# Per-head RMS norm and rotation of q and k: Sqrt and reciprocal replaced by Ln, Exp and one Newton step

## The chip, the core and the metric

The kernel runs on one core of one Trainium2 chip. The metric is device time of one execution in microseconds (us), lower is better. PE is TensorE, DVE is VectorE, ACT is ScalarE, POOL is GpSimd, SP is SyncE, which here only issues DMAs.

## What is computed

One encoder block: modulated RMS norm, an input projection, grouped-query attention beside a Fourier branch, gates, an output projection, then a GeGLU MLP. The change touches only the norm and rotation of q and k, which in the reference are:

```python
def rms_norm(x, g):
    xf = x.astype(jnp.float32)
    y = xf * lax.rsqrt(jnp.mean(xf * xf, axis=-1, keepdims=True) + NORM_EPS)
    return (y * g.astype(jnp.float32)).astype(x.dtype)
...
        h = rms_norm(x, mix_pre_g[l]) * (1.0 + scale1) + shift1
        z = h @ w_in[l]
        q = z[..., :o1].reshape(B, S, N_Q_HEADS, HEAD_DIM)
        k = z[..., o1:o2].reshape(B, S, N_KV_HEADS, HEAD_DIM)
...
        q = apply_rope(rms_norm(q, q_norm_g[l]), cos, sin)
        k = apply_rope(rms_norm(k, k_norm_g[l]), cos, sin)
```

There are 2048 positions, 8 query heads and 2 key heads of 64 channels, so q and k are 640 channels: 5 chunks of 128 channels (two heads each), each in 4 blocks of 512 positions. That is 20 blocks of 128x512 F32.

## The kernel before

`proj_phase` begins with six chunks of the projection: chunks 0 to 4 are q and k, chunk 5 is v. Then come 16 chunks of gates. PE makes a block by 24 matmuls of 128x512 (8 slices of the contraction, each a three-term hi/lo product, `product3`, L91 to L93) into one of four PSUM banks `ps[n]`. Block `i` is position block `n = i % 4` of chunk `c = i // 4`. For each of the 20 blocks of q and k the engines then do, in a pipeline whose order is written out by hand and whose joints are semaphores:

- ACT copies the block, times the gain, to `zg` (L888) and its square to `sq` (L889). It waits for the block's last product (`s_mm`) and, as `zg`, `sq`, `std` and `rot` have two slots each, for the end of block `i-2` (`s_rot`). With `hi_part` (L864), once a chunk, it rounds the weights of the next chunk.
- SP waits for `s_zg` and copies `zg` with neighbouring channels exchanged to `rot` by two DMAs (L693).
- PE takes the mean over each head's 64 channels by one F32 product with `head_mean` into `ps_ms` (L1017). It stands in PE's queue just ahead of the products of block `i+2`, and waits for `sq` and for the end of block `i-2`.
- ACT takes the root of mean + eps to `std` (`root`, L870, after the copies of block `i+1`).
- DVE multiplies by sin and cos and adds (L945, L946, L948), inverts `std` by a reciprocal (L950), makes the low part of the block before (L932, `rotated_lo`), and multiplies rotation and inverse root into `out` (L956), which posts `s_rot`. Once a chunk, L928 makes the low part of the next weights (`lo_part`).
- ACT rounds `out` of block `i-2` to `hi_st` (L876, `rotated_hi`), and POOL's queue stores both parts (L761, L763, `s_st`).

After block 19 ACT copies the four blocks of v (L907) into the buffers `out`, each when the stores from it have landed. PE turns them (L1038) and goes on with the gates, whose Sigmoids (L917) empty its PSUM banks.

Of the kernel before, what the change touches and what calls it, by code (L numbers as in the profile page):

```python
# [21 lines left out]
ALU = mybir.AluOpType  # L22
ACT = mybir.ActivationFunctionType
# [7 lines left out]
BLK = 512  # L31
NB = S // BLK
# [9 lines left out]
EPS = 1e-6  # L42
# [568 lines left out]
def proj_phase(nc, ahead, t_pos, w_z, w0, w0_at, hT_hi, hT_lo, b_gate, qk_g, rope_cos, rope_sin, head_mean_d, ident, f_d, f_stored, qk_d, gates_d,  # L611
# [7 lines left out]
    NROPE = NB * (NQC + 1)  # L619
# [6 lines left out]
    with Res(nc, "proj") as r:  # L626
        w_st, w_hi, w_lo = ([first] for first in w0)
        w_st.append(r.sb("w_st1", [P, KD, P]))
        for n, w in (("hi", w_hi), ("lo", w_lo)):
            r.sb(f"room_of_w_{n}0", [P, KD, P])  # L630
            w.append(r.sb(f"w_{n}1", [P, KD, P], F32R))
        out = r.sb("out", [P, NB, BLK])
# [13 lines left out]
        zg, sq, std, rot = (side[:, a, b * 2 * BLK:(b + 1) * 2 * BLK].rearrange("p (s q) -> p s q", s=2)  # L646
                            for a in (2, 3) for b in (0, 1))
# [3 lines left out]
        ps_ms = r.ps("ps_ms", [P, 2, BLK])  # L651
        ps_sw = r.ps("ps_sw", [P, 2, BLK])
        ps_m = [ps_ms, ps_sw, ps_b]
        ps = [ps_a[:, 0, :], ps_a[:, 1, :], ps_b[:, 0, :], ps_b[:, 1, :]]
        s_c, s_rt, s_eps = r.sem("consts"), r.sem("rotation_tables"), r.sem("eps_written")
        s_w = [r.sem(f"w_loaded{i}") for i in range(2)]
        s_hi, s_lo, s_mm, s_zg, s_ms, s_std, s_rot, s_out, s_rope = (
            r.sem(n) for n in ("w_hi_made", "w_lo_made", "products", "zg_sq", "mean", "root", "rotated", "v_or_gate", "rope"))
        s_sw = [r.sem(f"pairs_swapped{i}") for i in range(2)]
        s_rhi, s_rlo = r.sem("rotated_hi"), r.sem("rotated_lo")  # L660
        s_f, s_dft, s_z, s_zst = (r.sem(n) for n in ("f_loaded", "dft_steps", "z_split", "z_stored"))
# [5 lines left out]
        s_st = [r.pool_dma_sem(f"rotated_stored{n}") for n in range(NB)]  # L667
# [4 lines left out]
        for m in range(NG * NU):  # L672
            g, i = divmod(m, NU)
            n, k = divmod(i // UNITS * GROUPS_OF[g] * KD // -(-NU // UNITS), KD)
            units[NB * PER * g + FIRST_OF[g] + n][k].append(m)

        with r.block() as block:
# [182 lines left out]
            @block.scalar  # L860
            def _(act):
                def hi_part(c, i, u):
                    act.wait_ge(s_w[u], 16 * i + 16 * u)
                    act.activation(w_hi[u][:], w_st[u][:], ACT.Copy).then_inc(s_hi, 1)  # L864

                def root(c, n):
                    act.wait_ge(s_ms, 4 * c + n + 1)
                    if c or n >= 2:
                        act.wait_ge(s_rot, 4 * c + n - 1)
                    act.activation(std[:, n % 2, :], ps_ms[:, n % 2, :], ACT.Sqrt, bias=eps[:, 0:1]).then_inc(s_std, 1)  # L870

                def rotated_hi(i):
                    if i == 0:
                        f_stored(act)
                    act.wait_ge(s_rot, i + 1)
                    act.activation(hi_st[:, i % NB, :], out[:, i % NB, :], ACT.Copy).then_inc(s_rhi, 1)  # L876

                act.wait_ge(s_c, 16 * 3)
                act.wait_ge(s_eps, 1)
                for c in range(NQC + 1):  # L880
                    if c:
                        act.wait_ge(s_mm, 4 * c)
                    hi_part(c + 1, (c + 1) // 2, (c + 1) % 2)
                    for n in range(NB):
                        act.wait_ge(s_mm, 4 * c + n + 1)
                        if c or n >= 2:
                            act.wait_ge(s_rot, 4 * c + n - 1)
                        act.activation(zg[:, n % 2, :], ps[n], ACT.Copy, scale=gains[:, c:c + 1])  # L888
                        act.activation(sq[:, n % 2, :], ps[n], ACT.Square).then_inc(s_zg, 1)  # L889
                        if c or n >= 2:  # L890
                            rotated_hi(4 * c + n - 2)
                        if n:
                            root(c, n - 1)
                    root(c, NB - 1)

                def next_hi(c):
                    act.wait_ge(s_mm, 4 * c)
                    hi_part(c + 1, (c + 1) // 2, (c + 1) % 2)

                next_hi(NQC + 1)  # L900
                rotated_hi(NROPE - 2)
                for n in range(NB):
                    if n == 1:
                        rotated_hi(NROPE - 1)
                    act.wait_ge(s_mm, 4 * (NQC + 1) + n + 1)
                    act.wait_ge(s_st[n], STORED)
                    act.activation(out[:, n, :], ps[n], ACT.Copy).then_inc(s_out, 1)  # L907
                for j in range(2 * KD):
                    if NQKV + j + 1 < NC:
                        next_hi(NQKV + j)  # L910
                    for n in range(NB):
                        act.wait_ge(s_mm, 4 * (NQKV + j) + n + 1)
                        if j == 0:
                            act.wait_ge(s_tr, n + 1)
                        else:
                            act.wait_ge(s_gst[n], 16 * j)
                        act.activation(out[:, n, :], ps[n % 2], ACT.Sigmoid, bias=bg[:, j:j + 1]).then_inc(s_out, 1)  # L917
                        if j == 2 * KD - 1 and n == 2:
                            act.wait_ge(ahead.s_tp, 16)
                            act.wait_ge(s_un, NG * NU)  # L920
                            for k in range(ahead.K):
                                ahead.table_hi(act, k)

            @block.vector
            def _(dve):
                def lo_part(c, u):
                    dve.wait_ge(s_hi, c)
                    dve.tensor_tensor(w_lo[u][:], w_st[u][:], w_hi[u][:], ALU.subtract).then_inc(s_lo, 1)  # L928

                def rotated_lo(i):  # L930
                    dve.wait_ge(s_rhi, i + 1)
                    dve.tensor_tensor(out[:, i % NB, :].bitcast(F32R), out[:, i % NB, :], hi_st[:, i % NB, :],  # L932
                                      ALU.subtract).then_inc(s_rlo, 1)

                dve.memset(eps[:], EPS).then_inc(s_eps, 1)
                dve.wait_ge(s_rt, 16 * 2)
                for c in range(NQC + 1):
                    lo_part(c + 1, (c + 1) % 2)
                    for n in range(NB):
                        cols = slice(n * BLK, (n + 1) * BLK)  # L940
                        i = 4 * c + n
                        done = 4 * i
                        zc, rc, sc = zg[:, n % 2, :], rot[:, n % 2, :], std[:, n % 2, :]
                        dve.wait_ge(s_sw[n % 2], 32 * (i // 2 + 1))
                        dve.tensor_tensor(rc, rc, sin[:, cols], ALU.mult).then_inc(s_rope, 1)  # L945
                        dve.tensor_tensor(zc, zc, cos[:, cols], ALU.mult).then_inc(s_rope, 1)  # L946
                        dve.wait_ge(s_rope, done + 2)
                        dve.tensor_tensor(rc, rc, zc, ALU.add).then_inc(s_rope, 1)  # L948
                        dve.wait_ge(s_std, 4 * c + n + 1)
                        dve.reciprocal(sc, sc).then_inc(s_rope, 1)  # L950
                        if c or n:
                            rotated_lo(4 * c + n - 1)
                        dve.wait_ge(s_rope, done + 4)
                        if c:
                            dve.wait_ge(s_st[n], 32 * c)
                        dve.tensor_tensor(out[:, n, :], rc, sc, ALU.mult).then_inc(s_rot, 1)  # L956
                lo_part(NQKV, 0)
                rotated_lo(NROPE - 1)

                def split_v(n):  # L960
# [39 lines left out]
            def _(pe):  # L1000
# [10 lines left out]
                def rope_products(c, n):  # L1011
                    if c == 0 and n == 0:
                        pe.wait_ge(s_c, 16 * 3)
                    pe.wait_ge(s_zg, 4 * c + n + 1)
                    if c or n >= 2:
                        pe.wait_ge(s_rot, 4 * c + n - 1)
                    pe.matmul(ps_ms[:, n % 2, :], head_mean, sq[:, n % 2, :], start=True, stop=True).then_inc(s_ms, 1)  # L1017

                for c in range(NQC + 2):
                    if c:  # L1020
                        pe.wait_ge(s_lo, c)
                    for n in range(NB):
                        if c:
                            pe.wait_ge(s_zg, 4 * (c - 1) + n + 1)
                        if c <= NQC and n >= 2:
                            rope_products(c, n - 2)
                        if c and n < 2:
                            rope_products(c - 1, n + 2)
                        block_products(n, c % 2, n)
# [31 lines left out]
                for j in range(2 * KD):  # L1061
                    pe.wait_ge(s_lo, NQKV + j)
                    for n in range(NB):
                        i = NB * j + n
# [2196 lines left out]
```

## Time and profile before

| | |
|---|---|
| Median of 3 runs | 3081.8 us (3079.35 to 3087.96) |
| The profiled execution's own time | 3081.74 us |
| Its span | 3079.9 us |
| PE busy | 3002.9 us, 98% of the span |
| DVE busy | 2370.0 us, 77% |
| ACT busy | 1451.9 us, 47% |
| POOL busy | 574.8 us, 19% |
| Stage of q and k | first product at 160.3 us, last mean product at 298.9 us |

The time is 1.8 us more than the span, the stretch from the first to the last instruction. Busy times are sums over the whole span, and say nothing on a single stage. In the rows further down, the number after an instruction's start is its duration, and what stands in brackets is the engine's idle time before it and what ended it.

### The profile page before, as it was taken

How to read it: one execution, taken by the hardware profiler on the slowest of the kernel's cores; microseconds unless marked ns; L12 is line 12 of the kernel's file. 1: busy time of each engine (PE TensorE's matmuls, PEld its weight loads, DVE VectorE, ACT ScalarE, POOL GpSimd, SP SyncE). 2: the span in 40 equal slices, each digit the busy share in tenths (PEclk: the TensorE clock that was granted, in tenths of full speed). 3: DMA queues.
4: the chain of work that ended last, by engine and by line, in shares of the span. 5: the costliest groups of instructions: out<-in, count | busy, mean ns of one | idle time of the engine just before them, and what ended most of it. 6: DMA issues, size and time to landing. Idle time of an engine off the chain costs nothing.

```text
span 3079.9 us, 35419 instructions
## 1 busy us (share of the span) xinstructions
PE 3002.9 (98%) x13417; PEld 2418.7 (79%) x13417; DVE 2370.0 (77%) x2302; ACT 1451.9 (47%) x1856; POOL 574.8 (19%) x513
## 2 busy tenths in 40 slices
PE   5999999999999999999999999999999999999998
PEld 4777777777788888877888778888888888888887
DVE  6679687776499999997566789999564899996453
ACT  5433111111799999983333444444343444444433
POOL 0011522532000000000000244443120444440000
PEclk9999999999999999999999999999999999999999
DMA  8643332223721111148666332222664222226663
GB/s 338 216 150 135 130 112 80 86 100 124 228 52 38 35 39 35 39 128 248 188 218 218 132 110 82 82 83 82 218 215 166 93 82 83 82 83 218 215 211 126
DMA packets 159322, 408.11 MB, mean 133 GB/s; under 512 B 17992, under 2 KB 38472, under 8 KB 154664
## 3 DMA queue, kind: packets, MB, share of 16 engines
q1 hardware_dynamic: 141472, 352.88, 35.2%
q0 software_dynamic: 10192, 36.18, 3.1%
q10 hardware_dynamic: 7488, 16.78, 1.4%
q8 instruction: 107, 1.75, 0.2%
q14 instruction: 63, 0.52, 0.1%
HBM read 296.51 MB, written 104.02 MB: 130 GB/s over the span
## 4 chain that ended last, share of the span: by engine, by line
PE 66%; DVE 4%; ACT 1%; DMA 1%; issue 1%; POOL 0%; SPq 0%; ACTq 0%; DVEq 0%; POOLq 0%
PE second_ps_a L91 8%; PE second_ps_a L93 8%; PE second_ps_a L92 8%; PE second_ps_b L91 8%; PE second_ps_b L93 8%; PE second_ps_b L92 8%; PE att_ps_o L1597 7%; PE att_ps_s L1582 4%; PE att_ps_s L1583 4%; PE att_ps_r L1610 2%; DMA merge_x<-in_w_out 1%; PE att_ps_r L1615 0%; PE second_ps_b L1841 0%; DVE att_prob_lo L1519 0%; DVE ffn_x L2925 0%
## 5 line engine op out<-in xcount | busy, mean ns | idle before, releaser
L1519 DVE TENSOR_TENSOR att_prob_lo<-att_prob,att_prob_hi 128x1024 fp32r<-128x1024 f32 x256 | 309.9, 1221 | 24.1 <-ACT att_prob_hi L1479 22.9
L91 PE MATMUL second_ps_a<-up_in_hi,up_wu_hi 128*128 128x512 f32 x728 | 284.0, 390 | 5.1 <-DVE up_wu_lo L2375 3.1
L2911 DVE TENSOR_TENSOR ffn_wd_lo<-ffn_wd_st,ffn_wd_hi 128x1024 fp32r<-128x1024 f32 x110 | 130.6, 1224 | 201.9 <-ACT ffn_wd_hi L2734 201.9
L93 PE MATMUL second_ps_a<-up_in_hi,up_wu_lo 128*128 128x512 f32 x728 | 283.3, 389 | 0.0
L92 PE MATMUL second_ps_a<-up_in_lo,up_wu_hi 128*128 128x512 f32 x728 | 283.3, 389 | 0.0
L1479 ACT ACTIVATE att_prob_hi<-att_prob 128x1024 fp32r<-128x1024 f32 x256 | 272.2, 1064 | 0.0
L1473 ACT ACTIVATE att_prob<-att_ps_s 128x1024 f32<-128x1024 f32 x256 | 262.4, 1026 | 9.9 <-PE att_ps_s L1583 9.9
L2734 ACT ACTIVATE ffn_wd_hi<-ffn_wd_st 128x1024 fp32r<-128x1024 f32 x110 | 110.8, 1052 | 243.1 <-PE second_ps_a L93 132.1
L917 ACT ACTIVATE proj_out<-proj_ps,proj_bg 128x512 f32<-128x512 f32 x64 | 44.1, 689 | 378.2 <-PE proj_ps L93 365.5
L1597 PE MATMUL att_ps_o<-att_prob_hi,heads_kv 128*128 128x512 f32 x512 | 200.1, 391 | 1.8 <-DVE att_prob_lo L1519 1.7
L1597 PE MATMUL att_ps_o<-att_prob_lo,heads_kv 128*128 128x512 f32 x512 | 199.4, 389 | 0.0
L91 PE MATMUL second_ps_b<-up_in_hi,up_wu_hi 128*128 128x512 f32 x504 | 196.2, 389 | 0.0
L93 PE MATMUL second_ps_b<-up_in_hi,up_wu_lo 128*128 128x512 f32 x504 | 196.1, 389 | 0.0
L92 PE MATMUL second_ps_b<-up_in_lo,up_wu_hi 128*128 128x512 f32 x504 | 196.1, 389 | 0.0
L2015 POOL DMA_DIRECT2D scratch_x<-second_y x16 | 9.9, 620 | 966.0 <-DVE second_y L2199 966.0
L91 PEld LDWEIGHTS second_ps_a<-up_in_hi,up_wu_hi 128*128 128x128 f32 x728 | 136.6, 188 | 34.7 <-DVE up_wu_lo L2375 3.9
L93 PEld LDWEIGHTS second_ps_a<-up_in_hi,up_wu_lo 128*128 128x128 f32 x728 | 136.6, 188 | 28.5
L92 PEld LDWEIGHTS second_ps_a<-up_in_lo,up_wu_hi 128*128 128x128 f32 x728 | 136.7, 188 | 28.2
L2698 ACT ACTIVATE ffn_cv<-ffn_u,ffn_cw 128x1025 f32<-128x1025 f32 x88 | 109.8, 1248 | 99.3 <-issue 79.5
L91 PE MATMUL second_ps_b<-ffn_wd_hi,ffn_gs 128*128 128x512 f32 x396 | 154.3, 390 | 1.7 <-DVE ffn_gs L2907 1.7
L1533 DVE TENSOR_TENSOR att_acc<-att_acc,att_prob 128x1024 f32<-128x1024 f32 x128 | 155.9, 1218 | 0.0
L92 PE MATMUL second_ps_b<-ffn_wd_lo,ffn_gs 128*128 128x512 f32 x396 | 154.1, 389 | 0.0
(352 smaller groups left out, 8180.5 us busy)
## 6 DMA issues: line engine op xcount, KB each, us to landing
ffn_wd_st<-in_w_dn SPq DMA_DIRECT2D x110, 512.0 KB, 4.9
up_w_st<-in_w_up SPq DMA_DIRECT2D x44, 512.0 KB, 3.6
ffn_g_raw<-scratch_g SPq DMA_DIRECT2D x88, 192.0 KB, 4.2
scratch_gates<-proj_out SPq DMA_DIRECT2D x64, 256.0 KB, 2.0
early_w_st<-in_w_branch SPq DMA_DIRECT2D x32, 512.0 KB, 7.0
merge_gate<-scratch_gates SPq DMA_DIRECT2D x64, 256.0 KB, 3.7
up_w_st<-in_w_up SPq DMA_DIRECT2D x44, 256.0 KB, 4.1
up_w_a<-in_w_up SPq DMA_DIRECT2D x44, 256.0 KB, 4.3
```

The costliest lines, as they stand in the source:

```text
L91: pe.matmul(out, w_hi, x_hi, start=first, stop=False)
L92: pe.matmul(out, w_hi, x_lo, start=False, stop=False)
L93: return pe.matmul(out, w_lo, x_hi, start=False, stop=last)
L1473: act.activation(prob[:, s % RING, :], ps_s[:, s % 3, :], ACT.Exp, scale=SCALE).then_inc(s_exp, 1)
L1479: act.activation(prob_hi[:, s % LAG, :], prob[:, s % RING, :], ACT.Copy).then_inc(s_hi, 1)
L1519: dve.tensor_tensor(prob_lo[:, s % LAG, :], prob[:, s % RING, :], prob_hi[:, s % LAG, :], ALU.subtract)\
L1533: dve.tensor_tensor(at, at, prob[:, s % RING, :], ALU.add).then_inc(s_add, 1)
L1582: pe.matmul(at, kv[h % 2][:, 0, keys], q1[h % 2][:, cols], start=True, stop=False)
L1583: m = pe.matmul(at, kv[h % 2][:, 2, keys], q2[h % 2][:, cols], start=False, stop=True)
L1597: m = pe.matmul(ps_o[:], v, src[:, s % LAG, j * BLK:(j + 1) * BLK], start=t == 0 and part == 0, stop=t == NT - 1 and part == 1)
L2734: act.activation(wd_hi[split_at(m)][:], wd_st[staged_at(m)][:], ACT.Copy).then_inc(s_dhi, 1)
L2911: dve.tensor_tensor(wd_lo[split_at(m)][:], wd_st[staged_at(m)][:], wd_hi[split_at(m)][:], ALU.subtract).then_inc(s_dlo, 1)
```

## The change

The inverse root no longer comes from Sqrt and reciprocal. ACT now takes Ln of the mean, Exp of -0.5 times that, y, and the square of y, each waiting for the one before it. DVE makes one Newton step, y (1.5 - 0.5 m y^2), in two instructions. As eps can no longer be Sqrt's bias, DVE adds it to each square ahead of the mean product. On ACT the mean's instructions now come ahead of `rotated_hi` of block `i-2`. On DVE, the inverse root and the final product of block `i-1` come ahead of the rotation of block `i`. `s_zg` is now posted by the copy; the squares have a semaphore of their own. The mean stays one F32 product.

```diff
-                def root(c, n):
-                    act.wait_ge(s_ms, 4 * c + n + 1)
-                    if c or n >= 2:
-                        act.wait_ge(s_rot, 4 * c + n - 1)
-                    act.activation(std[:, n % 2, :], ps_ms[:, n % 2, :], ACT.Sqrt, bias=eps[:, 0:1]).then_inc(s_std, 1)
+                def inverse_root(i):
+                    at = std[:, i % 2, :]
+                    act.wait_ge(s_ms, i + 1)
+                    act.activation(at, ps_ms[:, i % 2, :], ACT.Ln).then_inc(s_std, 1)
+                    act.wait_ge(s_std, 3 * i + 1)
+                    act.activation(at, at, ACT.Exp, scale=-0.5).then_inc(s_std, 1)
+                    act.wait_ge(s_std, 3 * i + 2)
+                    act.activation(sq[:, i % 2, :], at, ACT.Square).then_inc(s_std, 1)
...
                     for n in range(NB):
-                        act.wait_ge(s_mm, 4 * c + n + 1)
-                        if c or n >= 2:
-                            act.wait_ge(s_rot, 4 * c + n - 1)
-                        act.activation(zg[:, n % 2, :], ps[n], ACT.Copy, scale=gains[:, c:c + 1])
-                        act.activation(sq[:, n % 2, :], ps[n], ACT.Square).then_inc(s_zg, 1)
-                        if c or n >= 2:
-                            rotated_hi(4 * c + n - 2)
-                        if n:
-                            root(c, n - 1)
-                    root(c, NB - 1)
+                        i = NB * c + n
+                        act.wait_ge(s_mm, i + 1)
+                        if i >= 2:
+                            act.wait_ge(s_rot, i - 1)
+                        act.activation(zg[:, n % 2, :], ps[n], ACT.Copy, scale=gains[:, c:c + 1]).then_inc(s_zg, 1)
+                        act.activation(sq[:, n % 2, :], ps[n], ACT.Square).then_inc(s_sq, 1)
+                        if i:
+                            inverse_root(i - 1)
+                        if i >= 2:
+                            rotated_hi(i - 2)
+                inverse_root(NROPE - 1)
...
+                def squares_eps(i):
+                    at = sq[:, i % 2, :]
+                    dve.wait_ge(s_sq, i + 1)
+                    dve.tensor_scalar(at, at, EPS, None, ALU.add).then_inc(s_sqeps, 1)
...
+                def newton(i, step):
+                    root, square = std[:, i % 2, :], sq[:, i % 2, :]
+                    if step == 0:
+                        dve.wait_ge(s_std, 3 * i + 3)
+                        dve.scalar_tensor_tensor(square, square, -0.5, ps_ms[:, i % 2, :], ALU.mult, ALU.mult).then_inc(s_nr, 1)
+                    else:
+                        dve.wait_ge(s_nr, 2 * i + 1)
+                        dve.scalar_tensor_tensor(root, square, 1.5, root, ALU.add, ALU.mult).then_inc(s_nr, 1)
...
                 for c in range(NQC + 1):
                     lo_part(c + 1, (c + 1) % 2)
-                        dve.wait_ge(s_std, 4 * c + n + 1)
-                        dve.reciprocal(sc, sc).then_inc(s_rope, 1)
...
+                    for i in range(NB * c, NB * (c + 1)):
+                        squares_eps(i)
+                        if i:
+                            newton(i - 1, 0)
+                        if i >= 2:
+                            rotated_lo(i - 2)
+                        if i:
+                            newton(i - 1, 1)
+                            normed(i - 1)
+                        rotate(i)
...
-                    pe.wait_ge(s_zg, 4 * c + n + 1)
+                    pe.wait_ge(s_sqeps, 4 * c + n + 1)
```

`rotate` holds the three instructions of L945 to L948 and `normed` the one of L956.

The next two fences are ACT's queue in the stage of q and k, one block long, first before the change. `proj_side` stands for each of `zg`, `sq`, `std`, `rot`, `cos` and `sin`, which lie in one buffer.

```order
L888 ACTIVATE proj_side<-proj_ps,proj_gains 128x512 [waits proj_rotated,proj_products]
L889 ACTIVATE proj_side<-proj_ps 128x512
L876 ACTIVATE proj_hi_st<-proj_out 128x512 [waits proj_rotated]
L870 ACTIVATE proj_side<-proj_ps_ms,proj_eps 128x512 [waits proj_rotated,proj_mean]
L888 ACTIVATE proj_side<-proj_ps,proj_gains 128x512 [waits proj_rotated,proj_products]
```

And with the change (L893 and L894 are the copy and the square, L870 Ln, L872 Exp, L874 the second Square, L880 `rotated_hi`):

```order
L893 ACTIVATE proj_side<-proj_ps,proj_gains 128x512 [waits proj_rotated,proj_products]
L894 ACTIVATE proj_side<-proj_ps 128x512
L870 ACT_TABLE_LOAD
L870 ACTIVATE proj_side<-proj_ps_ms 128x512 [waits proj_mean]
L872 ACT_TABLE_LOAD
L872 ACTIVATE proj_side<-proj_side 128x512 [waits proj_root]
L874 ACTIVATE proj_side<-proj_side 128x512 [waits proj_root]
L880 ACTIVATE proj_hi_st<-proj_out 128x512 [waits proj_rotated]
L893 ACTIVATE proj_side<-proj_ps,proj_gains 128x512 [waits proj_rotated,proj_products]
```

Four instructions became eight: besides Exp and Square the compiled program holds a table load ahead of Ln and another ahead of Exp, in each of the 20 blocks, and `rotated_hi` moved behind them.

DVE's queue over one block before the change (L932 is `rotated_lo`):

```order
L945 TENSOR_TENSOR proj_side<-proj_side 128x512 [waits proj_pairs_swapped0]
L946 TENSOR_TENSOR proj_side<-proj_side 128x512
L948 TENSOR_TENSOR proj_side<-proj_side 128x512 [waits proj_rope]
L950 RECIPROCAL proj_side<-proj_side 128x512 [waits proj_root]
L932 TENSOR_TENSOR proj_out<-proj_out,proj_hi_st 128x512 [waits proj_rotated_hi]
L956 TENSOR_TENSOR proj_out<-proj_side 128x512 [waits proj_rope]
```

And with it (L946 now adds eps, L961 and L964 are the Newton step, L937 `rotated_lo`, L971 the final product, L952 to L955 the rotation):

```order
L946 TENSOR_SCALAR proj_side<-proj_side 128x512 [waits proj_squares_steps]
L961 SCALAR_TENSOR_TENSOR proj_side<-proj_side,proj_ps_ms 128x512 [waits proj_root]
L937 TENSOR_TENSOR proj_out<-proj_out,proj_hi_st 128x512 [waits proj_rotated_hi]
L964 SCALAR_TENSOR_TENSOR proj_side<-proj_side 128x512 [waits proj_newton_steps]
L971 TENSOR_TENSOR proj_out<-proj_side 128x512 [waits proj_newton_steps,proj_rope]
L952 TENSOR_TENSOR proj_side<-proj_side 128x512 [waits proj_pairs_swapped1]
L953 TENSOR_TENSOR proj_side<-proj_side 128x512
L955 TENSOR_TENSOR proj_side<-proj_side 128x512 [waits proj_rope]
```

The reciprocal is gone, three instructions came in, and the final product of a block moved from behind its own rotation to ahead of the next block's.

## Rows read from the trace of the kernel before

**Rows 1.** The page: busy us, share of the span, instructions.

```profile
PE 3002.9 (98%) x13417; PEld 2418.7 (79%) x13417; DVE 2370.0 (77%) x2302; ACT 1451.9 (47%) x1856; POOL 574.8 (19%) x513
```

**Rows 2.** One chunk: us; PE, PEld, DVE, ACT, POOL busy; granted clock; DMA share, GB/s.

```profile
217.80:245.40 27.60, 26.05 (x106) 19.24 (x105) 26.52 (x26) 10.15 (x19) 4.34 (x8) 1.00 0.36 134
```

**Rows 3.** Waits, 155 to 326 us: waiter, releaser, total us, times, longest.

```profile
ACT proj_side L888 <- DVE proj_out L956: 79.2, 18, 7.1
...
PE proj_ps_ms L1017 <- ACT proj_side L889: 4.8, 10, 1.1
```

**Rows 4.** Timeline of DVE, one block: start us, us, instruction.

```profile
256.58 0.68 DVE L945 TENSOR_TENSOR proj_side<-proj_side 128x512 f32<-128x512 f32 x1
257.19 0.68 DVE L946 TENSOR_TENSOR proj_side<-proj_side 128x512 f32<-128x512 f32 x1
257.90 0.69 DVE L948 TENSOR_TENSOR proj_side<-proj_side 128x512 f32<-128x512 f32 x1
258.51 3.35 DVE L950 RECIPROCAL proj_side<-proj_side 128x512 f32<-128x512 f32 x1
261.78 0.63 DVE L932 TENSOR_TENSOR proj_out<-proj_out,proj_hi_st 128x512 fp32r<-128x512 f32 x1
262.32 0.68 DVE L956 TENSOR_TENSOR proj_out<-proj_side 128x512 f32<-128x512 f32 x1
```

**Rows 5.** Timeline of ACT over the same block.

```profile
255.62 0.69 ACT L888 ACTIVATE proj_side<-proj_ps,proj_gains 128x512 f32<-128x512 f32 x1 [4.64 <-DVE proj_out L956]
256.21 0.59 ACT L889 ACTIVATE proj_side<-proj_ps 128x512 f32<-128x512 f32 x1
256.69 0.63 ACT L876 ACTIVATE proj_hi_st<-proj_out 128x512 fp32r<-128x512 f32 x1
257.21 0.69 ACT L870 ACTIVATE proj_side<-proj_ps_ms,proj_eps 128x512 f32<-128x512 f32 x1
263.09 0.69 ACT L888 ACTIVATE proj_side<-proj_ps,proj_gains 128x512 f32<-128x512 f32 x1 [5.20 <-DVE proj_out L956]
```

**Rows 6.** Timeline of PE: mean products of blocks 0, 5 and 19.

```profile
171.29 1.02 PE L1017 MATMUL proj_ps_ms<-proj_side,proj_small 128*128 128x512 f32 x2
...
202.86 1.02 PE L1017 MATMUL proj_ps_ms<-proj_side,proj_small 128*128 128x512 f32 x2
...
298.85 1.10 PE L1017 MATMUL proj_ps_ms<-proj_side,proj_small 128*128 128x512 f32 x2 [0.16 <-ACT proj_side L889]
```

**Rows 7.** Timeline of ACT at a table load elsewhere, in the MLP.

```profile
1767.31 0.58 ACT L2679 ACTIVATE ffn_p<-second_ps_a 128x512 f32<-128x512 f32 x1
1767.91 1.28 ACT L2704 ACT_TABLE_LOAD   x1
1769.20 1.06 ACT L2704 ACTIVATE ffn_cv<-ffn_cv 128x1025 f32<-128x1025 f32 x1
```

**Rows 8.** Groups by line and shape: count, busy us, mean ns.

```profile
L1825 DVE TENSOR_SCALAR second_y<-second_y,second_stats 128x1024 f32<-128x1024 f32 x10 | 7.0, 750 | 0.0
L2940 DVE SCALAR_TENSOR_TENSOR ffn_x<-ffn_y_g,ffn_rstd,ffn_x 128x512 f32<-128x512 f32 x2 | 1.4, 750 | 0.0
```

**Rows 9.** Timelines at the stage's begin: ACT's copy of block 1, DVE's first low part.

```profile
171.49 0.69 ACT L888 ACTIVATE proj_side<-proj_ps,proj_gains 128x512 f32<-128x512 f32 x1 [2.80 <-PE proj_ps L93]
...
171.70 1.23 DVE L928 TENSOR_TENSOR proj_w_lo<-proj_w_st,proj_w_hi 128x1024 fp32r<-128x1024 f32 x1 [11.31 <-DMA proj_side<-in_rope_sin]
```

**Rows 10.** Timelines behind the stage: last final product, v, first Sigmoid, v turned.

```profile
310.03 0.68 DVE L956 TENSOR_TENSOR proj_out<-proj_side 128x512 f32<-128x512 f32 x1
...
322.53 0.60 ACT L907 ACTIVATE proj_out<-proj_ps 128x512 f32<-128x512 f32 x1 [6.57 <-DMA scratch_qk<-proj_out]
...
325.39 0.69 ACT L917 ACTIVATE proj_out<-proj_ps,proj_bg 128x512 f32<-128x512 f32 x1
...
327.54 0.60 PE L1038 MATMUL proj_ps_sw<-keep_ident,proj_out 128*128 128x128 f32 x4
```

**Rows 11.** Columns as in rows 2, for a stretch of the first phase.

```profile
60.00:80.00 20.00, 16.14 (x81) 13.17 (x80) 14.83 (x17) 15.56 (x25) 0.00 (x0) 0.91 0.53 185
```

More of the change, by code:

```diff
@@ L658, in proj_phase @@
             r.sem(n) for n in ("w_hi_made", "w_lo_made", "products", "zg_sq", "mean", "root", "rotated", "v_or_gate", "rope"))
+        s_sq, s_sqeps, s_nr = (r.sem(n) for n in ("squares_steps", "squares_eps", "newton_steps"))
         s_sw = [r.sem(f"pairs_swapped{i}") for i in range(2)]
@@ L936, in _, with rotate @@
                 dve.wait_ge(s_rt, 16 * 2)
+                def squares_eps(i):
+                    at = sq[:, i % 2, :]
+                    dve.wait_ge(s_sq, i + 1)
+                    dve.tensor_scalar(at, at, EPS, None, ALU.add).then_inc(s_sqeps, 1)
+                def rotate(i):
+                    cols = slice(i % NB * BLK, (i % NB + 1) * BLK)
+                    zc, rc = zg[:, i % 2, :], rot[:, i % 2, :]
+                    dve.wait_ge(s_sw[i % 2], 32 * (i // 2 + 1))
+                    dve.tensor_tensor(rc, rc, sin[:, cols], ALU.mult).then_inc(s_rope, 1)
+                    dve.tensor_tensor(zc, zc, cos[:, cols], ALU.mult).then_inc(s_rope, 1)
+                    dve.wait_ge(s_rope, 3 * i + 2)
+                    dve.tensor_tensor(rc, rc, zc, ALU.add).then_inc(s_rope, 1)
@@ L937, in _, with normed @@
+                def normed(i):
+                    dve.wait_ge(s_rope, 3 * i + 3)
+                    dve.wait_ge(s_nr, 2 * i + 2)
+                    if i >= NB:
+                        dve.wait_ge(s_st[i % NB], 32 * (i // NB))
+                    dve.tensor_tensor(out[:, i % NB, :], rot[:, i % 2, :], std[:, i % 2, :], ALU.mult).then_inc(s_rot, 1)
                 for c in range(NQC + 1):
                     lo_part(c + 1, (c + 1) % 2)
[L939 to L948, printed above, removed]
-                        dve.wait_ge(s_std, 4 * c + n + 1)
-                        dve.reciprocal(sc, sc).then_inc(s_rope, 1)
[L951 to L956, printed above, removed]
@@ L957, in _ @@
+                    for i in range(NB * c, NB * (c + 1)):
[8 more added lines that the diff above has]
+                        rotate(i)
                 lo_part(NQKV, 0)
+                newton(NROPE - 1, 0)
+                rotated_lo(NROPE - 2)
@@ L958, in _ @@
+                newton(NROPE - 1, 1)
+                normed(NROPE - 1)
                 rotated_lo(NROPE - 1)
@@ L1013, in rope_products @@
                         pe.wait_ge(s_c, 16 * 3)
-                    pe.wait_ge(s_zg, 4 * c + n + 1)
+                    pe.wait_ge(s_sqeps, 4 * c + n + 1)
                     if c or n >= 2:
                         pe.wait_ge(s_rot, 4 * c + n - 1)
-                    pe.matmul(ps_ms[:, n % 2, :], head_mean, sq[:, n % 2, :], start=True, stop=True).then_inc(s_ms, 1)
+                    at = ps_ms[:, n % 2, :]
+                    pe.matmul(at, head_mean, sq[:, n % 2, :], start=True, stop=True).then_inc(s_ms, 1)
                 for c in range(NQC + 2):
@@ L1023, in _ @@
                         if c:
-                            pe.wait_ge(s_zg, 4 * (c - 1) + n + 1)
+                            pe.wait_ge(s_sq, 4 * (c - 1) + n + 1)
                         if c <= NQC and n >= 2:
```

## The prediction

> **What bounds the kernel now.** I read the page first: PE is busy for 98% of the span [rows 1], so a change away from PE pays or costs only where PE comes to wait for it. Then the stretches: over one chunk of q and k (27.60 us) PE is busy 26.05, DVE 26.52 and ACT 10.15 [rows 2]. This is the only stage in which DVE is as full as PE. The waits say who is late. ACT's copy of a block waits 18 times, 79.2 us in all, for DVE's final product two blocks back, and PE waits 10 times, 4.8 us, for the squares that ACT makes behind that copy [rows 3]. The reader is to see a ring in rows 4 and 5: DVE's final product of a block lets ACT start on the block after the next, and DVE goes from that product straight to the next rotation. Its queue sets the pace: 0.61 for the sin product, 0.71, 0.61, then 3.27 for the reciprocal, 0.54 and 0.60, start to start, about 6.34 us for a block, and with the waits for the root and one `lo_part` a chunk 27.6/4 = 6.90 [rows 2, 4]. PE by itself is only a little faster: mean product 0 starts at 171.29 and product 5 at 202.86, so PE unhindered needs 6.31 us a block; the last starts at 298.85 [rows 6]. At PE's own pace it would start at 171.29 + 19 x 6.31 = 291.2. So 7.7 us is all that any change of this stage can gain. A measurement of this kernel can tell about 0.3% (9.2 us) from no change, so "faster" is nearly out of reach before the change is looked at.
>
> **DVE gets lighter.** The reciprocal goes (3.27 of queue). Three instructions come in. Two are SCALAR_TENSOR_TENSOR on 128x512. The nearest rows are 0.68 for a two-input product and 0.75 for this operation with a scalar read from memory [rows 4, 8]; the scalars here are immediates, so I take 0.72, with 0.68 and 0.75 as ends. The third adds eps, TENSOR_SCALAR 128x512. The row is 0.75 for 128x1024, so between half of that, 0.38, and the 0.68 of the two-input product. I take 0.45, since a fixed part doesn't halve. Queue time per block: 6.34 - 3.27 + 2 x 0.63 + 0.36 = 4.7 us. DVE is no longer the bound, by 1.6 us against PE.
>
> **ACT gets two table loads a block.** ACT's queue with the change has a load before Ln and one before Exp, 40 in all; the trace of before has none in this stage. The row elsewhere shows what one costs: the instruction ahead ends at 1767.89, the load starts at 1767.91, takes 1.28, and the next starts at 1769.20 [rows 7]. So 1.29 for the load, 0.02 for the wait until the engine has run dry, and the overlap of about 0.1 between neighbours (0.58 start to start for an instruction of 0.69 [rows 5]) is lost too. The load doesn't wait for data, so it could hide in idle time. But both stand between ACT's squares of block `i` and DVE's Newton step of block `i-1`, and the ring runs through just there.
>
> A rule of the Trainium skill speaks of this price ("ScalarE: Activation LUTs", What ACT_TABLE_LOAD costs): 1283 ns for the load and some 1380 ns of drain, 2.66 us for every switch to another set. The trace agrees on the 1.28 and not on the drain: 0.02 us after the end of what stood ahead. By the page's price the sum below would be higher by 2 x 1.38 x 18 = 50 us.
>
> **The ring, step by step.** Start T(i) is ACT's copy of block `i`. DVE's iteration `i` ends the ring with the final product of block `i-1`, for which ACT's copy of block `i+1` waits. From rows 4, 5 and 7:
>
> - copy, 0.58 to the next start, and square, 0.59: 1.17
> - dry, 0.02, and first load, 1.29: 2.48
> - Ln of 128x512 out of PSUM. Square with the same operands takes 0.59, Sqrt with a pointer for its bias 0.69; no pointer shows in the queue, so 0.59: 3.07. Its mean is long there, as that product runs behind the products of block `i`.
> - dry and second load, 1.31: 4.38
> - Exp, from SBUF, as the 0.63 of L876: 5.01
> - 0.04 for a dependence inside the engine (L948 starts 0.03 after the end of L946 [rows 4]; I allow up to 0.1). Square, 0.63, and 0.03 to DVE, by the same row: 5.71
> - first Newton instruction, 0.63 to the next start: 6.34. By then `rotated_hi`, which starts 0.52 behind the second Square, is done too (6.21).
> - `rotated_lo`, 0.54: 6.88
> - second Newton instruction, 0.72 + 0.03: 7.63
> - final product, 0.68, and 0.10 to ACT (262.32 + 0.68 to 263.09 [rows 4, 5]): 8.41
>
> The ends: 8.3 with 0.68 for the Newton instructions and no dependence cost; 8.65 with Ln at 0.69, Newton at 0.75 and 0.1 for each dependence. The rest hides. `hi_part`, some 1.05 a chunk, fits in ACT's idle time from 6.2 to 8.4. Rotation, `lo_part` and eps add on DVE (1.93 + 1.13 + 0.36) are done 3.3 us after T, while DVE waits for ACT until 5.7. PE needs 6.31 of 8.41, so it now waits about 2.1 us a block, at its mean product, for the eps add.
>
> So a period of 8.41 in place of 6.90. PE gained with the reciprocal what it can't use, and the loads take it back twice over: without them the ring would be 8.41 - 2.6 = 5.8, below PE's 6.31.
>
> **The sum.** T(1) stays at 171.49 [rows 9]; block 1 hangs on PE alone. T(19) = 171.49 + 18 x 8.41 = 322.9. The first mean product is late, as eps add 0 stands behind `lo_part`, which waits for the rotation tables until 171.70 [rows 9]: 171.70 + 1.13 + 0.45 + 0.08 = 173.4 in place of 171.29, 2 us of PE time. That runs beside the ring and costs at most 0.4 there. Mean product 19 waits for rotation 18 and eps add 19: 322.9 + 1.75 + 0.45 + 0.08 = 325.2, against 298.85 [rows 6]. **Late by 26.3 us.**
>
> Behind it PE runs as before: blocks of v, first gates. The slack there gets smaller. The last final product now ends at about T(19) + 15.4 = 338.3 (two more loads, `hi_part` and `lo_part` stand before it), 27.6 later than 310.71, so 1.3 more than PE. The first Sigmoid ended at 326.08, while PE had turned the second block of v at 328.14 [rows 10]. Of these 2.1 us 1.3 go, and 0.8 is left. If it isn't, up to 3 us are lost. From there on everything moves by the same amount, for PE bounds the rest.
>
> Against the profiled execution's own 3081.74 us, which is the median to 0.1: 3081.7 + 26.3 = **3108.0 us**. The ring's ends move it by 18 x (-0.11 to +0.24) = -2 to +4.3, the slack by up to +3, the scatter of the runs of before (3079.4 to 3088.0) by some 3 to either side: 3101 to 3117.
>
> **Rivals.**
>
> *The loads are not what the chip does twice a block (other side, not slower).* If Ln and Exp lay in one table set that also serves Copy and Square, a single load would stand at the stage's begin. The ring would be 5.8, PE the bound at 6.31, and the last mean product at 173.4 + 19 x 6.31 = 293.3: 5.6 us gained, 3076, within 0.3%. It decides from a ring below 6.9 us, that is with fewer than 1.5 us of loads in it; with one load a block the ring is 7.1, and the time 3086. For it: only the names of the functions. Against it: the program of the change holds 40 loads, and those that the trace of before shows stand where its program has them. 3%, and 1% for the one load a block.
>
> The Trainium skill has the rule ("ScalarE: Activation LUTs", Table sets: the hidden batching unit): the set `natural_log_exp_and_others` has both, so Ln and then Exp cost one load. By it this rival would hold; no run of before shows either function beside the other.
>
> *The switch is dearer when it goes to and fro.* All loads in the trace stand alone, with long stretches between. If two in quick turn cost a further 1.38 each, the period is 11.2 and the time 3108 + 50 = 3158. For it no row of this trace; against it, the load itself has one length, 1.28 [rows 7]. 3%.
>
> *PE's clock falls.* PE will be busy for three quarters of this stage, with a gap in each block. In a stretch of the first phase with 16.14 busy of 20 us the granted clock was 0.91, so part of it ran at 1.2 GHz [rows 11]; at 0.94 busy it was 1.00 [rows 2]. A short fall is covered by PE's 2.1 us a block. If the clock stayed at 1.2 GHz, PE would need 2 x 6.31 = 12.6 a block and be the bound: 19 x 4.2 = 80 us on top, 3188. 3%.
>
> **Chances.** The forecast, two loads a block in a ring of 8.3 to 8.65, has 90% and gives 3101 to 3117. Rivals as said: 4% for fewer loads (within 0.3%), 3% for dearer switches, 3% for the clock. Since the smallest of the slower cases is 19 us off, three times the scatter, slower by over 0.3% has 0.95, within 0.3% 0.04, faster 0.01. The range takes one more us at each end for joints of ACT that no row shows: 3100 to 3118.
>
> **What would show it.** Table loads: 40 of 1.28 us between the first product and the v blocks, each starting 0.02 after the instruction ahead. Copies of ACT 8.4 us apart, waiting for the final product. DVE busy under 20 us in 34 and waiting on the second Square. PE waiting about 2 us a block at the mean product. No TABLE_LOAD there, or a period under 7, would prove me wrong in the main step; a period near 11 would give the second rival, and a clock under 0.8 with PE always busy the third.

## The result, and the profile after

The changed kernel takes 3114.3 us (median of 4 runs, 3111.7 to 3115.6) against 3081.1 us before: a ratio of 1.0094, with an interval of 1.0082 to 1.0106, so slower by 25 to 33 us. The quotient of these two medians is 1.0108 (33.2 us) and lies just outside that interval: with 4 runs to a side the size is less sure than the direction. Measured again, it took 3111.7 us (4 runs) against 3084.0 (15 runs), ratio 1.0087, 1.0071 to 1.0102. The forecast of 3081.7 + 26.3 us is a ratio of 1.0085, inside both intervals; 3114.3 is inside the range too, and 6 us above the number given.

The page of the changed kernel, its span and busy times:

```profile
span 3113.6 us, 35525 instructions
...
PE 3006.3 (97%) x13417; PEld 2420.5 (78%) x13417; DVE 2338.3 (75%) x2342; ACT 1527.5 (49%) x1936; POOL 570.3 (18%) x513
```

PE does the same 13417 matmuls. ACT has 76 us more, of which the loads are 51, and DVE 32 us less: work was taken from the engine that was full, and the kernel got slower. The same 27.6 us stretch as in [rows 2], columns as there:

```profile
217.80:245.40 27.60, 22.02 (x90) 16.30 (x89) 16.48 (x27) 20.98 (x28) 3.36 (x7) 1.00 0.29 105
```

PE fell from 26.05 us busy to 22.02, DVE from 26.52 to 16.48, and ACT rose from 10.15 to 20.98. No engine is full: this is what a ring of waits (each engine waits for another, and the last for the first) looks like in sums. The timeline of ACT over one block (start us, us, instruction), to be held against [rows 5]:

```profile
255.76 0.69 ACT L893 ACTIVATE proj_side<-proj_ps,proj_gains 128x512 f32<-128x512 f32 x1 [2.28 <-DVE proj_out L971]
256.35 0.59 ACT L894 ACTIVATE proj_side<-proj_ps 128x512 f32<-128x512 f32 x1
256.95 1.28 ACT L870 ACT_TABLE_LOAD   x1
258.25 0.60 ACT L870 ACTIVATE proj_side<-proj_ps_ms 128x512 f32<-128x512 f32 x1
258.86 1.28 ACT L872 ACT_TABLE_LOAD   x1
260.16 0.63 ACT L872 ACTIVATE proj_side<-proj_side 128x512 f32<-128x512 f32 x1
260.82 0.63 ACT L874 ACTIVATE proj_side<-proj_side 128x512 f32<-128x512 f32 x1
261.36 0.61 ACT L880 ACTIVATE proj_hi_st<-proj_out 128x512 fp32r<-128x512 f32 x1
261.88 1.05 ACT L865 ACTIVATE first_w_hi<-h_w_st 128x1024 fp32r<-128x1024 f32 x1
264.25 0.69 ACT L893 ACTIVATE proj_side<-proj_ps,proj_gains 128x512 f32<-128x512 f32 x1 [1.33 <-DVE proj_out L971]
```

Copy to copy is 8.49 us. The weights' part at 261.88 only shortens ACT's idle time, from 2.28 to 1.33. DVE's half of a ring, one block (the last row lets ACT start at 213.28):

```profile
206.53 0.42 DVE L946 TENSOR_SCALAR proj_side<-proj_side 128x512 f32<-128x512 f32 x1
210.51 0.69 DVE L961 SCALAR_TENSOR_TENSOR proj_side<-proj_side,proj_ps_ms 128x512 f32<-128x512 f32 x1 [3.56 <-ACT proj_side L874]
211.12 0.68 DVE L937 TENSOR_TENSOR proj_out<-proj_out,proj_hi_st 128x512 fp32r<-128x512 f32 x1
211.72 0.68 DVE L964 SCALAR_TENSOR_TENSOR proj_side<-proj_side 128x512 f32<-128x512 f32 x1
212.49 0.69 DVE L971 TENSOR_TENSOR proj_out<-proj_side 128x512 f32<-128x512 f32 x1
```

In this block DVE waits 3.56 us for ACT's second Square. The waits of the stage (155 to 356 us), in place of [rows 3]:

```profile
DVE proj_side L961 <- ACT proj_side L874: 60.6, 19, 3.6
...
ACT proj_side L893 <- DVE proj_out L971: 37.4, 18, 2.3
```

Each waits for the other once a block, ACT less than before (37.4 us for 79.2), DVE 60.6 us in 19 waits, 3.2 each. PE's mean products 0 and 19, for [rows 6]:

```profile
172.56 1.10 PE L1050 MATMUL proj_ps_ms<-proj_side,proj_small 128*128 128x512 f32 x2 [1.79 <-DVE proj_side L946]
...
326.00 1.10 PE L1050 MATMUL proj_ps_ms<-proj_side,proj_small 128*128 128x512 f32 x2 [1.75 <-issue]
```

The last one starts 27.15 us later than before (326.00 - 298.85). The spans differ by 33.7.

### The profile page after: what moved, and what is told of

Its sections match the earlier page's. It is cut to its first block, busy times and chain, and to the rows that moved or that the text cites. A ratio compares the mean times of both kernels' runs of the same rounds, so it can differ in the third digit from the quotient of the medians.

```text
span 3113.6 us, 35525 instructions
## 1 busy us (share of the span) xinstructions
PE 3006.3 (97%) x13417; PEld 2420.5 (78%) x13417; DVE 2338.3 (75%) x2342; ACT 1527.5 (49%) x1936; POOL 570.3 (18%) x513
## 4 chain that ended last, share of the span: by engine, by line
PE 66%; DVE 4%; ACT 1%; DMA 1%; issue 1%; POOL 0%; SPq 0%; ACTq 0%; DVEq 0%; POOLq 0%
PE second_ps_a L91 8%; PE second_ps_a L93 8%; PE second_ps_a L92 8%; PE second_ps_b L91 8%; PE second_ps_b L93 8%; PE second_ps_b L92 8%; PE att_ps_o L1630 7%; PE att_ps_s L1615 4%; PE att_ps_s L1616 4%; PE att_ps_r L1643 2%; DMA merge_x<-in_w_out 1%; PE att_ps_r L1648 0%; PE second_ps_b L1874 0%; DVE att_prob_lo L1552 0%; DVE ffn_x L2958 0%
## 5 line engine op out<-in xcount | busy, mean ns | idle before, releaser
L93 PEld LDWEIGHTS second_ps_a<-up_in_hi,up_wu_lo 128*128 128x128 f32 x728 | 136.6, 188 | 28.4
L92 PEld LDWEIGHTS second_ps_a<-up_in_lo,up_wu_hi 128*128 128x128 f32 x728 | 136.7, 188 | 28.4
L91 PE MATMUL second_ps_b<-ffn_wd_hi,ffn_gs 128*128 128x512 f32 x396 | 154.2, 389 | 1.7 <-DVE ffn_gs L2940 1.7
L93 PE MATMUL second_ps_b<-ffn_wd_hi,ffn_gs 128*128 128x512 f32 x396 | 154.1, 389 | 0.0
```

What stands on the lines that cost most here:

```text
L91: pe.matmul(out, w_hi, x_hi, start=first, stop=False)
L92: pe.matmul(out, w_hi, x_lo, start=False, stop=False)
L93: return pe.matmul(out, w_lo, x_hi, start=False, stop=last)
```

## The experiments

The theory is that the two loads stand on the ring. Its rivals are that the new order or the longer chain costs, or that the number of loads costs, wherever they are. Four kernels decide between them, and a fifth tests what one of them showed besides. The stage is read by the start of its last mean product.

**One set.** One load of the set that holds both functions, asked for by name at the head of the stage:

```diff
+                act.preload_act_table_set("natural_log_exp_and_others")
                 act.wait_ge(s_c, 16 * 3)
```

> The changed kernel with one added table load at the head of the stage of q and k, of the set that holds Ln and Exp together; no load stands in the blocks any more. Everything else, the eps add and the Newton step too, is as in the changed kernel. My theory (the two loads a block stand on the ring from ACT's copy to DVE's final product): the ring falls from 8.50 us by two times 1.31 and the regained overlap of 0.1 to about 5.8, under PE's own 6.31 us, so PE sets the pace. Last mean product at about 293 (298.9 before, 326.0 changed), time about 3076 us. Rival (the new order and the longer chain of ACT and DVE, not the loads, are what costs): the period stays above 6.9 and the time at or above that of before.

Measured: 3082.5 us (11 runs) against 3083.2 (33 runs), ratio 0.9989 (0.9979 to 1.0000). ACT over a block, no load in it:

```profile
250.97 0.69 ACT L894 ACTIVATE proj_side<-proj_ps,proj_gains 128x512 f32<-128x512 f32 x1 [2.80 <-PE proj_ps L93]
251.55 0.59 ACT L895 ACTIVATE proj_side<-proj_ps 128x512 f32<-128x512 f32 x1
252.03 0.60 ACT L870 ACTIVATE proj_side<-proj_ps_ms 128x512 f32<-128x512 f32 x1
252.66 0.63 ACT L872 ACTIVATE proj_side<-proj_side 128x512 f32<-128x512 f32 x1
253.33 0.63 ACT L874 ACTIVATE proj_side<-proj_side 128x512 f32<-128x512 f32 x1
...
257.28 0.69 ACT L894 ACTIVATE proj_side<-proj_ps,proj_gains 128x512 f32<-128x512 f32 x1 [2.80 <-PE proj_ps L93]
```

The copy now waits for PE, no longer for DVE: 6.31 us a block, PE's own pace. All of the slowdown is gone with the loads and nothing else changed, so neither the order nor the longer chain was the cause. The time missed its expectation of 3076 by 6.5 us. About 2 us of that are in the stage (294.96 in place of 293), at its begin:

```profile
173.27 1.93 PE L1051 MATMUL proj_ps_ms<-proj_side,proj_small 128*128 128x512 f32 x2 [2.78 <-DVE proj_side L947]
...
175.84 0.63 PE L93 MATMUL proj_ps<-h_hi,first_w_lo 128*128 128x512 f32 x1
176.27 0.63 PE L91 MATMUL proj_ps<-h_hi,first_w_hi 128*128 128x512 f32 x1
...
294.96 1.02 PE L1051 MATMUL proj_ps_ms<-proj_side,proj_small 128*128 128x512 f32 x2
```

PE had waited 2.78 us for the first eps add, and then ran for a while at 1.2 GHz: matmuls 0.43 us apart (175.84 to 176.27) in place of 0.23. A stretch of the same profile around it shows the granted clock at 0.66 (the number ahead of the DMA share):

```profile
172.00:177.00 5.00, 3.73 (x8) 2.30 (x9) 3.44 (x6) 1.71 (x3) 0.00 (x0) 0.66 0.26 98
```

That cost 1.7 us beside the wait: mean product 1 comes 8.05 after mean product 0 (181.32), not 6.31. The kernel with two idle loads, further down, shows the same: a wait of 2.43, the fall, and 8.00.

**One load a block on the ring.** The same call just ahead of each Ln, none at the head.

```diff
+                    act.preload_act_table_set("natural_log_exp_and_others")
                     act.wait_ge(s_ms, i + 1)
                     act.activation(at, ps_ms[:, i % 2, :], ACT.Ln).then_inc(s_std, 1)
```

> The changed kernel with the joint set of Ln and Exp loaded anew just ahead of each Ln: one load a block in place of two, at the same place of the ring. My theory (each load on the ring costs its whole 1.3 to 1.4 us a block): period 7.2 us, last mean product at about 303, time about 3086 us, halfway between none and two loads if the part below PE's pace is left out. Rival (a load hides behind something, or only the switch to and fro is dear): period at or below 6.9, or still near 8.5.

Measured: 3093.5 us (10 runs) against 3083.2, ratio 1.0032 (1.0022 to 1.0042). Two copies of ACT and what stands between them, shortened:

```profile
236.55 0.69 ACT L894 ACTIVATE proj_side<-proj_ps,proj_gains 128x512 f32<-128x512 f32 x1 [2.28 <-DVE proj_out L972]
...
237.75 1.28 ACT L869 ACT_TABLE_LOAD   x1
239.04 0.60 ACT L871 ACTIVATE proj_side<-proj_ps_ms 128x512 f32<-128x512 f32 x1
...
243.77 0.69 ACT L894 ACTIVATE proj_side<-proj_ps,proj_gains 128x512 f32<-128x512 f32 x1 [2.28 <-DVE proj_out L972]
```

The period is 7.22 us, the last mean product starts at 303.74, both as expected. From one load to two the period grows by 8.49 - 7.22 = 1.27. The whole missed its expectation of 3086 by 7.5 us. Against before it is 10.3 us slower, of which the stage has 4.9 (303.74 - 298.85); the other 5.4 are behind it (see below).

**Two loads a block in ACT's idle time.** One set, and behind `rotated_hi` in each block a load of another set and one back.

```diff
                         if i >= 2:
                             rotated_hi(i - 2)
+                        act.preload_act_table(ACT.Sigmoid)
+                        act.preload_act_table_set("natural_log_exp_and_others")
```

> As with one set for Ln and Exp, but with two loads in each block again, of another set and back, placed behind the part that rounds the rotated block, where ACT would be idle. As many loads as in the changed kernel (41 against 40), but off the ring. My theory: ACT's queue gets 6.15 us a block long, 6.4 with the weights' part, so the period is 6.3 to 6.5 and the time 3076 to 3081 us. Rival (what costs is the number of loads, wherever they stand): 26 us or more above before, as the changed kernel.

Measured: 3079.8 us (10 runs) against 3083.2, ratio 0.9985 (0.9976 to 0.9994). The loads are there, 41 in the stage where the changed kernel has 40, and ACT's queue has no gap left:

```profile
241.03 0.62 ACT L880 ACTIVATE proj_hi_st<-proj_out 128x512 fp32r<-128x512 f32 x1
241.66 1.28 ACT L900 ACT_TABLE_LOAD   x1
242.95 1.28 ACT L901 ACT_TABLE_LOAD   x1
244.25 1.06 ACT L865 ACTIVATE first_w_hi<-h_w_st 128x1024 fp32r<-128x1024 f32 x1
245.21 0.67 ACT L894 ACTIVATE proj_side<-proj_ps,proj_gains 128x512 f32<-128x512 f32 x1
```

The last mean product starts at 294.46, with one set at 294.96. So 51 us of table loads cost nothing in one place and 31 us of the stage (326.00 - 294.96) in another. The rival that counts loads falls.

**The order alone.** The new order with Sqrt (eps as bias) and reciprocal, no eps add, no Newton step.

```diff
-                        squares_eps(i)
...
+                    act.activation(std[:, i % 2, :], ps_ms[:, i % 2, :], ACT.Sqrt, bias=eps[:, 0:1]).then_inc(s_std, 1)
...
+                        dve.wait_ge(s_std, i + 1)
+                        dve.reciprocal(std[:, i % 2, :], std[:, i % 2, :]).then_inc(s_nr, 1)
```

> The order of the changed kernel (inverse root and final product of the block before come ahead of the rotation) with the old functions: Sqrt with eps as its bias and the reciprocal, no eps add, no Newton step. My theory: the reciprocal no longer waits for the root (0.47 us in half of the blocks before), and DVE's queue of 6.4 us a block plus the low part of the weights gives a period of 6.7 in place of 6.9; last mean product about 295, time about 3078 us, which is within the noise of before. Rival (the order costs): period above 6.9 and a longer time than before.

Measured: 3080.5 us (11 runs) against 3083.2, ratio 0.9989 (0.9978 to 0.9999). The last mean product started at 293.17, where that of before started at 298.85. DVE, from the low part of the weights on:

```profile
246.64 1.22 DVE L928 TENSOR_TENSOR first_w_lo<-h_w_st,first_w_hi 128x1024 fp32r<-128x1024 f32 x1
247.77 3.35 DVE L955 RECIPROCAL proj_side<-proj_side 128x512 f32<-128x512 f32 x1
251.04 0.63 DVE L932 TENSOR_TENSOR proj_out<-proj_out,proj_hi_st 128x512 fp32r<-128x512 f32 x1
```

The reciprocal starts as soon as DVE is free. The new order gains about 4 us of the stage by itself (this profile's stage also began 1.3 us earlier), so it can't be what made the change slow.

**eps in the Ln.** One set, and the eps add taken away: the late first mean product and the fall of the clock behind it should go with it.

```diff
-                        squares_eps(i)
...
-                    act.activation(at, ps_ms[:, i % 2, :], ACT.Ln).then_inc(s_std, 1)
+                    act.activation(at, ps_ms[:, i % 2, :], ACT.Ln, bias=eps[:, 0:1]).then_inc(s_std, 1)
...
-                        dve.scalar_tensor_tensor(square, square, -0.5, ps_ms[:, i % 2, :], ALU.mult, ALU.mult).then_inc(s_nr, 1)
+                        dve.scalar_tensor_tensor(square, ps_ms[:, i % 2, :], EPS, square, ALU.add, ALU.mult).then_inc(s_nr, 1)
```

> One table set for Ln and Exp, and no eps add on DVE: eps is Ln's bias and is added once more in the first Newton instruction; the second Square carries a factor of 0.5 and a sign moves to the final product, so DVE has three instructions of 0.69 where the kernel with one set has three and the add. Mean product 0 waits for ACT's squares alone again. My theory: no wait of 2.8 us at mean product 0 and no fall of PE's clock behind it, PE at its own 6.31 us from first to last: last mean product about 291 (295.0 with one set alone), time about 3 to 4 us under that of one set alone in the stage, some 7.5 us under before, about 3075 us. Rival (the pointer for the bias lengthens the ring past PE, or the clock falls anyway): no better than one set alone, some 3 us under before.

Measured: 3079.3 us (11 runs) against 3084.0 (15 runs), ratio 0.9982 (0.9973 to 0.9991): faster than both kernels, than that of before by only 0.2%. Its first and last mean product:

```profile
170.89 1.02 PE L1050 MATMUL proj_ps_ms<-proj_side,proj_small 128*128 128x512 f32 x2
...
290.84 1.02 PE L1050 MATMUL proj_ps_ms<-proj_side,proj_small 128*128 128x512 f32 x2
```

119.95 us for 19 blocks, 6.31 each, with no wait: the 7.7 us that the prediction called all that can be gained in this stage (127.56 before). Only 4.8 arrive in the medians.

**The same kernels again**, for the 6.6 us that the stage doesn't explain: a second profile of the changed kernel, a second and a third of before and of eps in the Ln.

> The changed kernel unchanged, for a second profile of it. The stage of q and k explains 27.1 of the 33.7 us by which the two profiles' spans differ. My theory for the other 6.6: falls of PE's granted clock at stage borders, which come and go from run to run and are not the change's; so the second profile has the same period of 8.50 us and the same 27 us in the stage, but other falls behind it, and another remainder. Rival (the change does something to the later stages): the same remainder of 6 to 7 us at the same places.

> The kernel before, for a second profile of it. If the falls of the granted clock come and go by themselves, this one has other falls behind the stage of q and k than the first, and its span differs from 3079.9 us by about 1.7 us for each stretch of half clock more or less. If they belong to the kernel, it has the same three.

> The kernel with eps in Ln once more, for its profile. In its first profile 8.1 us were gained by the end of the stage of q and k and only 2.4 by the end of the span; the clock fell at 767, 812, 1375 and 1426 us. If these falls come and go by themselves, the stage shows the same -8 us again and the rest other falls; if they belong to this kernel, the same ones stand there again and eat the same 5 to 6 us.

> The same kernel a third time, with the same two readings: the stage at -8 us in any case; the falls behind it the same as in the first profile if they belong to the kernel, others if they don't.

> The kernel before a third time, beside them. Its first two profiles had falls at 76, 1380 and 1431 us in common, the second two more at 1773 and 1804. If falls vary from run to run, the set differs again; by the other reading 76, 1380 and 1431 stay.

Measured: spans of 3113.6 and 3110.6 us for the changed kernel, 3079.9, 3084.0 and 3082.5 for that of before, 3077.5, 3078.6 and 3077.5 for eps in the Ln. The table gives how much later (+) than in the first profile of before the same DVE instruction starts, for instructions that stood at these times before:

| profile | 760 us | 1000 us | 1480 us | 2100 us | 3000 us |
|---|---|---|---|---|---|
| before, second | 0.1 | 0.2 | 0.2 | 4.3 | 4.1 |
| before, third | -0.2 | 1.2 | 1.8 | 2.7 | 2.6 |
| changed | 27.2 | 30.5 | 33.0 | 33.9 | 33.7 |
| changed, second | 28.4 | 31.3 | 29.4 | 30.9 | 30.7 |
| one set | -4.2 | -1.3 | 0.8 | 0.8 | 0.7 |
| one load | 4.9 | 5.5 | 9.1 | 12.0 | 11.9 |
| two idle loads | -4.7 | -4.5 | -4.4 | -4.4 | -4.1 |
| order alone | -5.7 | -5.8 | -8.9 | -7.4 | -7.5 |
| eps in the Ln | -8.3 | -5.4 | -2.2 | -2.2 | -2.5 |
| eps in the Ln, second | -4.3 | -1.5 | -3.6 | -1.2 | -1.4 |
| eps in the Ln, third | -8.7 | -5.9 | -5.5 | -2.5 | -2.4 |

The first column is the stage of q and k. (In the second profile of eps in the Ln it began 3.9 us later and took the same 120.0 us.) Behind it the kernel of before moves by 4.0 and 2.7 us against its own first profile; the changed kernel moves by 6.5 and 2.3, one load by 7.0, eps in the Ln by 5.8, 2.9 and 6.3. The profile that all are held against is the quietest of the three of before: behind the stage its clock fell twice (the very end aside), in the others four times each. Where time is lost, the clock often fell; a fall here is a stretch that the profile records at half the clock, 1.2 GHz. In the changed kernel's first profile, for instance, just behind the border to the Fourier stage:

```profile
800.00:810.00 10.00, 8.58 (x54) 8.39 (x55) 2.96 (x6) 2.66 (x5) 0.00 (x0) 0.83 0.83 294
```

The granted clock was 0.83 there; in the profile of before no fall is recorded between 80 and 1379 us. The falls behind the stage stood at 802, 846, 1410 and 1461 in the one profile of the changed kernel, at 846 and 1802 in the other; before had 1380 and 1431 each time, with 1773 and 1804 in the second, 773 and 1763 in the third. Eps in the Ln had 767, 812, 1375 and 1426 in the first, 814 and 1797 in the second, and in the third those of the first (766, 811, 1374, 1425) with 1756 and 1797. So part of them varies with the run and part comes again, and the two readings in the expectations are not told apart.

The steps of the table do go with the falls. Between 760 and 1000 us the clock fell in both profiles of the changed kernel, in one set and in all three of eps in the Ln, and each lost 2.8 to 3.3 us there. The third of before had one fall and lost 1.3. One load, two idle loads, order alone and the other two of before had none and moved by 0.6 or less. Ahead of every fall behind the stage PE had just waited 1.7 us or more, but for the one near 1380 (1410 in the changed kernel), where it had gaps of up to 1.0. Why such a place gets a fall in one run and not in another, and whether the change has a part in it, stays open: with two profiles of the changed kernel it can't be ruled out.

In the second profile of the changed kernel the clock also fell within the stage:

```profile
200.00:260.00 60.00, 49.71 (x185) 36.20 (x185) 35.70 (x59) 44.32 (x59) 7.55 (x14) 0.94 0.27 103
```

Its mean product 19 started 154.94 us after mean product 0, in the first profile 153.44. Five falls stand in that stretch, at 174, 218, 235, 269 and 303 us. The first cost the 1.5 us: mean product 1 came 8.00 after mean product 0, in the first profile 6.40. The next lap of the ring then waited for PE:

```profile
180.52 0.69 ACT L893 ACTIVATE proj_side<-proj_ps,proj_gains 128x512 f32<-128x512 f32 x1 [3.86 <-PE proj_ps L93]
```

The other four cost nothing, since the ring kept its 8.50 us a block: PE's waits covered them.

## Why the prediction was right

- **What bounds the stage.** Before, DVE's queue; no change of this stage could gain more than 7.7 us. Right: eps in the Ln reaches PE's pace and gains 7.6 (127.56 to 119.95).
- **DVE is lighter, and it is no use.** The Newton instructions took 0.69 (0.72 assumed), the eps add 0.42 (0.45). DVE was busy 16.48 of 27.6 us.
- **The loads' price.** 1.28 each, beginning 0.02 behind the instruction ahead, to and fro as well as alone. The period fell by 1.27 when one went. The 1380 ns of drain that the Trainium skill adds ("ScalarE: Activation LUTs", What ACT_TABLE_LOAD costs) appear in none of the 40; the rival with a dearer switch (3158 us) is out.
- **The ring.** 8.41 forecast, 8.50 measured. ACT's part is right to 0.02. The difference is on DVE: `rotated_lo` took 0.60 to the next start (0.54 assumed), and 0.77 passed between the second Newton instruction and the product, where 0.75 was assumed. Times 18 it is 1.6 us. As the stage also began 0.7 us earlier than before (its first product at 159.62 us), the last mean product was late by 27.15 and not by 27.9.
- **The first mean product** was late, by the wait of 1.79 us; in the first profile it cost the ring nothing to speak of, as forecast. What was missed is that the clock can fall behind such a wait. Where it fell there, block 1 took 1.6 to 1.7 us longer: in one set, with two idle loads, and also in the second profile of the changed kernel. "A short fall is covered by PE's 2.1 us a block" held for the four falls further on, not for this one.
- **PE's wait** was forecast for the eps add, at the mean product. PE waited at 17 mean products, 31.2 us in all; the profile puts 5 of these waits down to the eps add and names no releaser for the other 12.
- **Behind the stage** the first Sigmoid ended at 353.50 and PE had turned the second block of v at 355.28: 1.8 us of slack left, 0.8 forecast. Nothing was lost there.
- **The rival of the shared set** was priced rightly in the stage (last mean product 293.3 forecast, 294.96 measured, the clock between them), less so in the whole (3076 for 3082.5), and didn't hold for the kernel as built. With one load a block the prediction has a ring of 7.1 and 3086; its own sum gives 3084.4 for that ring, and the runs gave 7.22 and 3093.5. The Trainium skill is right that one set has both functions ("ScalarE: Activation LUTs", Table sets: the hidden batching unit); but the kernel gets it only when that set is asked for by name. From the names of the functions alone the loads alternated.
- **The size.** 3114.3 against 3108.0. The profile's 33.7 us are 7.4 more than the forecast: 0.8 of them lie in the stage (27.15 for 26.3), the other 6.6 behind it. Two of its four falls there (802 and 846) have no counterpart in the first profile of before, and the second profile of the changed kernel has only 2.3 us behind the stage. The second measurement (27.7 between the medians) is within 1.4 us of the forecast, the first (33.2) 6.9 off. How near the total comes is thus in part luck; the 27.15 of the stage are not.

The step that was too narrow is the allowance for scatter, "some 3 to either side": the runs named there already reach 6.3 us above the profiled one, and profiles of one and the same kernel differ by up to 4 us behind this stage. Nor do the terms of the range add up to its ends: they give 3103 to 3118, not 3101 to 3117. The result lies inside either.

## What to carry to other kernels

Look for table loads in the compiled order before counting instructions: two functions that share a set on paper may still be loaded from two. A load costs its 1.3 us only on a ring or path that sets the pace; in idle time 40 of them cost nothing. And relieving the full engine gains no more than the distance to the next bound: when the work moves onto another engine, add up the ring through both, as neither needs to be full.

## What was unexpected

- A wait of 2.0 to 2.8 us of a PE that was busy before can be followed by a stretch at 1.2 GHz (granted clock 0.66 over 5 us, matmuls 0.43 us apart in place of 0.23). It was so at 173 to 174 us in one set, with two idle loads and in the second profile of the changed kernel, after 2.78, 2.43 and 2.03 us, and not in the changed kernel's first profile, after 1.79, nor with one load, after 2.33. So the length of the wait alone doesn't decide it:

```profile
172.32 1.10 PE L1050 MATMUL proj_ps_ms<-proj_side,proj_small 128*128 128x512 f32 x2 [2.03 <-DVE proj_side L946]
...
172.18 1.09 PE L1051 MATMUL proj_ps_ms<-proj_side,proj_small 128*128 128x512 f32 x2 [2.33 <-DVE proj_side L947]
```

  The first row is of the changed kernel's second profile, the second of one load.
- A gain of 8 us early in the kernel arrived as 5 in the medians. One set and order alone likewise gained 4 to 6 us in the stage and 0.7 and 2.7 between the medians; one load lost 5 there and 10 over all. The ratios stand; why the later stages mostly take a bit back isn't settled.
